# Causal attention on one core: mask, row maximum and sign folded into one VectorE instruction, transposes one unit later, PSUM copies divided between ScalarE and VectorE

## What is computed

```python
s = einsum('bhqd,bhkd->bhqk', qi, k) * scale          # FOX: + cum[t] - cum[s]
s = where(kpos <= qpos, s, -inf)
p = softmax(s, axis=-1)
out = einsum('bhqk,bhkd->bhqd', p, v)
```

## Time and profile before

| what | value |
|---|---|
| median of 3 runs | 2117.88 us |
| the profiled execution's own time | 2119.32 us |
| its span in the trace | 2117.4 us |
| PE busy over the span | 2027.0 us (96%) |
| VectorE, ScalarE, POOL busy | 988.1, 482.2, 336.7 us |
| granted PE clock, mean | 0.985 |

### The profile page before, as it was taken

The page is one execution under the profiler, slowest core; times in us unless marked ns, Lnnn a source line. Parts: engine busy times, 40 slices in busy tenths (PEclk is TensorE's granted clock), DMA queues, the critical chain, the costliest instruction groups (busy, mean ns, idle before and its releaser), DMA issues. The chain is left out here.

```text
span 2117.4 us, 20496 instructions
## 1 busy us (share of the span) xinstructions
PE 2027.0 (96%) x7494; PEld 1086.0 (51%) x7494; DVE 988.1 (47%) x1833; ACT 482.2 (23%) x1142; POOL 336.7 (16%) x474
## 2 busy tenths in 40 slices
PE   8999999999999999999899999999998999999995
PEld 4444444579874445444445456454445556544442
DVE  2444544557672124333454656253344467534333
ACT  1111111023341001100331147220004447520000
POOL 1000000001011000333100013103331003203333
PEclk9999999999999999999999999999999999999998
DMA  5223365510022124799636830138994120045996
GB/s 187 87 97 129 119 250 185 210 52 1 1 90 90 61 80 159 266 402 403 240 113 213 312 136 1 44 141 320 405 391 147 62 102 1 3 158 203 371 377 253
DMA packets 123511, 363.30 MB, mean 172 GB/s; under 512 B 27597, under 2 KB 33001, under 8 KB 110865
## 3 DMA queue, kind: packets, MB, share of 16 engines
q1 hardware_dynamic: 77856, 174.13, 23.4%
q10 hardware_dynamic: 30432, 157.30, 18.9%
q0 software_dynamic: 15120, 30.53, 4.1%
HBM read 335.60 MB, written 43.52 MB: 179 GB/s over the span
## 5 line engine op out<-in xcount | busy, mean ns | idle before, releaser
L1617 PE MATMUL bank<-ring,work 128*128 128x512 f32 x768 | 342.5, 599 | 3.3 <-DVE work L1633 3.3
L1617 PEld LDWEIGHTS bank<-ring,work 128*128 128x128 f32 x768 | 143.8, 192 | 168.1 <-issue 168.1
L1916 POOL DMA_INDIRECT work<-x_rows,small x168 | 169.2, 1007 | 269.8 <-DVE work L1881 197.3
L1628 PE MATMUL bank<-ring_halves,work 128*128 128x512 f32 x384 | 172.8, 593 | 4.0 <-DVE work L1642 4.0
L432 PE MATMUL bank<-featT,ring 128*128 128x512 f32 x384 | 170.4, 597 | 2.4 <-DMA ring<-in_w_in 2.4
L1345 PE MATMUL bank<-ring,work 128*128 128x512 f32 x384 | 168.2, 598 | 3.3 <-PEq L2182 2.2
L2396 PE MATMUL bank<-ring,featT 128*128 128x512 f32 x384 | 169.0, 601 | 1.6 <-DVE small L2485 1.6
L1639 DVE TENSOR_TENSOR work<-work,bank 128x256 f32<-128x256 f32 x48 | 20.2, 421 | 282.3 <-ACT work L1636 282.3
L2396 PEld LDWEIGHTS bank<-ring,featT 128*128 128x128 f32 x384 | 73.6, 193 | 93.9 <-issue 92.2
L1628 PEld LDWEIGHTS bank<-ring_halves,work 128*128 128x128 f32 x384 | 72.7, 190 | 95.1 <-issue 95.1
L1345 PEld LDWEIGHTS bank<-ring,work 128*128 128x128 f32 x384 | 72.8, 192 | 92.5 <-issue 92.5
(11 more groups left out here) (443 smaller groups left out, 2808.1 us busy)
## 6 DMA issues: line engine op xcount, KB each, us to landing
ring<-in_w_in SPq DMA_DIRECT2D x15, 2048.0 KB
ring<-in_moe_w_gate ACTq DMA_DIRECT2D x28, 1024.0 KB
ring<-in_moe_w_up ACTq DMA_DIRECT2D x28, 1024.0 KB
ring_halves<-in_moe_w_down ACTq DMA_DIRECT2D x28, 1024.0 KB, 10.3
ring_halves<-in_w_ada SPq DMA_DIRECT2D x48, 512.0 KB, 6.3
y_rows<-work ACTq DMA_DIRECT2D x48, 512.0 KB
ring<-in_expert_w_gate ACTq DMA_DIRECT2D x14, 1024.0 KB
ring<-in_expert_w_up ACTq DMA_DIRECT2D x14, 1024.0 KB
```

The costliest lines, as they stand in the source:

```text
L1617: last = nc.tensor.matmul(gu_sum[par], xgT[par][:, k, :], w_gu[par][:, k, :, :], start=(k == 0), stop=(k == KD - 1))
L1628: last = nc.tensor.matmul(bank[5 + h][:, :], hT[par][:, k, :], w_dn[par][:, k, span(h)], start=(k == 0), stop=(k == KF - 1))
L1916: nc.gpsimd.indirect_dma_start(out=xg[par][:, s * QD:(s + 1) * QD], out_offset=None, in_=x_quarters, in_offset=bass.IndirectOffsetOnAxis(a ...
```

## The change

The first VectorE instruction now does all three things: it adds a 512-column mask (zeros, then the triangle) to all the scores, multiplies by -1 (FOX) or by minus the row factor (MLA), writes the result back to PSUM and gives its minimum as accumulator output. ScalarE's exponent takes the scale -1.0 in both. turn moves from 3 to 4 units behind S, ScalarE's copy pT from step i + 1 to step i + 3, and the ring of pT from 4 to 6. The two long units' pT (t = 3) and the out copy go to VectorE. pv(j) moves to step 2j + 7, out(p) to 8p + 16. ScalarE's copy of a turned q stands one step before its PE step instead of two.

```diff
-        N_SX, N_PT = 6, 4
+        N_SX, N_PT = 6, 6
-            mask = scr[:, N_PT * BANK:N_PT * BANK + P]
+            mask = scr[:, N_PT * BANK:(N_PT + 1) * BANK]
-            TURN_LAG = 3
-            AHEAD = TURN_LAG - 1
+            TURN_LAG = 4
+            AHEAD = 1
+            KEEP_LAG = 3
-            pv_at = {2 * j + 5: j for j in range(N // 2)}
-            out_at_step = {PER_PAIR * p + 10: p for p in pairs}
+            pv_at = {2 * j + 7: j for j in range(N // 2)}
+            out_at_step = {PER_PAIR * p + 16: p for p in pairs}
+            by_dve = [t == T - 1 for _, t in units]
+            pT_kept = lambda j: DV if by_dve[j] else AC
...
@@ PE
-                                AC.wait(pe, ("pT", j - 2))
+                                pT_kept(j - 2).wait(pe, ("pT", j - 2))
...
@@ ScalarE
-                            DV.wait(act, ("neg" if q_root is None else "scaled", i))
+                            DV.wait(act, ("neg", i))
-                                                         scale=1.0 if q_root is None else q_root[:, at:at + 1], accum_out=inv[:, i:i + 1]), ("exp", i))
+                                                         scale=-1.0, accum_out=inv[:, i:i + 1]), ("exp", i))
-                        if 1 <= i < N + 1:
-                            j = i - 1
+                        if KEEP_LAG <= i < N + KEEP_LAG and not by_dve[i - KEEP_LAG]:
+                            j = i - KEEP_LAG
...
@@ VectorE
-                            DV.done(nc.vector.tensor_tensor(d, d, mask, ALU.add), ("mask", i))
-                            DV.wait(dve, ("mask", i))
-                            DV.done(nc.vector.reduce_max(mx[:, i:i + 1], bank[i % N_S][:, 0:(t + 1) * P], X_AXIS, negate=True), ("neg", i))
-                            if q_root is not None:
-                                at = t * NHB + h
-                                DV.wait(dve, ("neg", i))
-                                DV.done(nc.vector.tensor_tensor(mx[:, i:i + 1], mx[:, i:i + 1], q_root[:, at:at + 1], ALU.mult), ("scaled", i))
+                            DV.done(nc.vector.tensor_tensor_reduce(scores, scores, mask[:, (T - 1 - t) * P:T * P], -1.0 if minus_root is None else minus_root[:, at:at + 1],
+                                                                   3.0e38, ALU.add, ALU.min, mx[:, i:i + 1]), ("neg", i))
+                        if i in out_at_step:
+                            p = out_at_step[i]
+                            PE.wait(dve, ("pv", T * p + T - 1))
+                            DV.done(nc.vector.tensor_copy(outT[:, p, :], bank[6 + p % 2][:, :]), ("out", p))
...
+                        if TURN_LAG <= i < N + TURN_LAG and by_dve[i - TURN_LAG]:
+                            j = i - TURN_LAG
...
+                            DV.done(nc.vector.tensor_copy(pT[j % N_PT][:, 0:n, :], bank[4 + j % 2][:, 0:n * P].rearrange("p (s n) -> p s n", s=n)), ("pT", j))
```

More of the change, by code:

```diff
@@ L2137, in build, with attention @@
         TURNED_HEADS = 4
-        N_SX, N_PT = 6, 4
-        def attention(dk, q, k, v, turned_at, out_at, q_root, k_gain):
+        N_SX, N_PT = 6, 6
+        def attention(dk, q, k, v, turned_at, out_at, minus_root, k_gain):
             scr = featT[:, :, :].rearrange("p k s -> p (k s)")
@@ L2175, in attention @@
                 ac_n += [("exp", i)] if i < N else []
-                ac_n += ([("q", q_at[i + AHEAD])] if i + AHEAD in q_at else []) + ([("out", out_at_step[i])] if i in out_at_step else [])
-                ac_n += [("pT", i - 1)] if 1 <= i < N + 1 else []
+                ac_n += ([("q", q_at[i + AHEAD])] if i + AHEAD in q_at else [])
+                ac_n += [("pT", i - KEEP_LAG)] if KEEP_LAG <= i < N + KEEP_LAG and not by_dve[i - KEEP_LAG] else []
                 dv_n += [("k", k_at[i])] if i in k_at else []
-                dv_n += ([("mask", i), ("neg", i)] + ([] if q_root is None else [("scaled", i)])) if i < N else []
-                dv_n += [("inv", i - 1)] if 1 <= i < N + 1 else []
+                dv_n += [("neg", i)] if i < N else []
+                dv_n += ([("out", out_at_step[i])] if i in out_at_step else []) + ([("inv", i - 1)] if 1 <= i < N + 1 else [])
+                dv_n += [("pT", i - TURN_LAG)] if TURN_LAG <= i < N + TURN_LAG and by_dve[i - TURN_LAG] else []
             stage(pe_n, ac_n, dv_n, ["mask0", "mask"] + [("share", i) for i in range(N)])
@@ L2223, in _ @@
                             p, t = j // T, j % T
-                            AC.wait(pe, ("pT", 2 * j + 1))
+                            for m in range(2):
+                                pT_kept(2 * j + m).wait(pe, ("pT", 2 * j + m))
                             if t == 0 and p >= 2:
-                                AC.wait(pe, ("out", p - 2))
+                                DV.wait(pe, ("out", p - 2))
                             for s in range(t + 1):
@@ L2289, in _ @@
                             DV.done(nc.vector.reciprocal(inv[:, i - 1:i], inv[:, i - 1:i]), ("inv", i - 1))
+                        if TURN_LAG <= i < N + TURN_LAG and by_dve[i - TURN_LAG]:
+                            j = i - TURN_LAG
+                            n = units[j][1] + 1
+                            PE.wait(dve, ("turn", j))
+                            if j >= N_PT:
+                                PE.wait(dve, ("pv", (j - N_PT) // 2))
+                            DV.done(nc.vector.tensor_copy(pT[j % N_PT][:, 0:n, :], bank[4 + j % 2][:, 0:n * P].rearrange("p (s n) -> p s n", s=n)), ("pT", j))
                 @block.gpsimd
@@ L2294, in _ @@
                     PO.wait(pool, "mask0")
-                    PO.done(nc.gpsimd.affine_select(out=mask, in_=mask, compare_op=ALU.is_ge, fill=-3.0e38, base=0, pattern=[[-1, P]], channel_multiplier=1), "mask")
+                    PO.done(nc.gpsimd.affine_select(out=mask[:, (T - 1) * P:T * P], in_=mask[:, (T - 1) * P:T * P], compare_op=ALU.is_ge, fill=-3.0e38, base=0,
+                                                    pattern=[[-1, P]], channel_multiplier=1), "mask")
                     for i, (h, t) in enumerate(units):
@@ L2916, in _ @@
                 AC.wait(dve, "q_exp")
-                DV.done(V.scalar_tensor_tensor(out=T4(q_root, NHB), in0=T4(q_root, NHB), scalar=QK ** -0.5, in1=per_t(q_inv), op0=ALU.mult, op1=ALU.mult), "q_root")
+                DV.done(V.scalar_tensor_tensor(out=T4(q_root, NHB), in0=T4(q_root, NHB), scalar=-QK ** -0.5, in1=per_t(q_inv), op0=ALU.mult, op1=ALU.mult), "q_root")
             @block.gpsimd
```

10 lines of the change are left out of this document (3 added, 7 removed).

## The result

The changed kernel takes 2097.73 us (median of 5 runs, 2096.70 to 2103.16) against 2117.88 us. The medians differ by 20 us, where 14.5 were forecast. Over all runs the ratio is 0.9912, 95% interval 0.9896 to 0.9929, and by it the change is worth 18.6 us (15.0 to 22.0).

What follows compares the result with a forecast made beforehand. PE was taken to set the pace, with waits of 0.69 us (FOX) and 1.05 (MLA) a pair; 4.8 + 7.4 + 1.4 + 1.6 + 0.8 - 1.5 = 14.5 us off 2117.88 gave 2103.4 us, range 2098.5 to 2110.

Steps and rivals of the forecast that it cites:

- forecast case: Both attentions: PE's waits on share go, 14.5 us off the median to 2103.4 us; chance 0.72.
- low end of the range: Whole kernel at 2098.5: accumulator for nothing and no new wait, 3 us, and 1 to 2 for small waits not counted.
- Waits of pairs 1 to 7: PE's waits on share in FOX and MLA pairs, 0.69 and 1.05 us each, all gone: 4.8 and 7.4 us.
- What removes them: Share chain: the turn a unit later gives 1.45 us more cover against waits of at most 0.64.
- the tie on ScalarE: ScalarE's queue: pT(i - 1) waits for turn(i - 1) at PE's step i + 2, before exp(i + 1), delaying the next exponent.
- The new instruction: Fused VectorE step: 0.69 us for 512 columns, 0.75 with a factor from memory, plus 0.16 for the accumulator.
- What is late next: VectorE's second long pT copy, 4.0 us against PE's 3.9: 0.1 us a pair, 1.5 us given back.
- First pair and moved work: Block start: first-pair waits 0.7 us in each attention, work moved behind S(63) 0.8 in each; 1.4 + 1.6 us.
- Tail: Chain of unit 63 at each block's end: 0.3 us gained in FOX, 0.5 in MLA, together 0.8.
- VectorE's queue gives part back: Waits move to VectorE's copies, 0.5 us a pair, 6 us more given back: 2109.5; chance 0.15.
- VectorE becomes the bound: Fused instruction at two clocks an element, VectorE 12.8 us a FOX pair, 13.3 MLA: slower, 2124; chance 0.08.
- PE was not waiting: The 0.69 and 1.05 us are PE's own cost between unlike groups; only the ends gain: 2115.6; chance 0.05.

Runs made afterwards that it cites:

- lags alone: Kernel before with only the later turn, pT, pv and out, six pT tiles and nearer q copy; three VectorE instructions, copies on ScalarE: 2106.97 us, ratio 0.9948.
- pv by two: Changed kernel with two pv standing together at step 2j + 7 of the second, 2 groups a pair instead of 4: 2100.32 us, ratio 0.9914.
- extra pass: Changed kernel with one more VectorE maximum over the same columns, result unread, in front of every fused instruction: 2113.37 us, one run.

## Why the prediction was right or wrong

The direction and the forecast case were right. The time of 2103.4 us was 5.7 us above the median, and 4.2 us of gain were missing in the two blocks. The median lies 0.8 us under the low end of the range (2098.5); the ratio gives 2099.2. A part of the mechanism was wrong, and luck hid it: the change contained both parts that the gain needs. By its steps:

- *Waits of pairs 1 to 7*: 4.8 and 7.4 us, from 0.69 and 1.05 a pair. The pairs fell by 0.66 and 1.05, the middles by 84.39 - 79.33 = 5.1 and 87.15 - 79.18 = 8.0. The start-to-start reading, and 11.60 us as PE's own price, were right to 0.04.
- *What removes them*: wrong. The prediction gave it all to the lags and counted the fused instruction only in the tail. The lags alone leave 0.17 us a pair in FOX and 0.67 in MLA; the fused instruction is worth 8.2 us on top of them. The comparison of 1.45 us of cover with waits of at most 0.64 looked at the share chain only, though the prediction named the tie on ScalarE. With the share covered, the copy that frees the transposes' bank was late next. The tie itself was read rightly: one step of it costs 0.43 us a pair.
- *The new instruction*: 0.69 and 0.75 taken, 0.699 and 0.758 measured; accumulator 0.16 taken, 0.141 measured. VectorE's sum of 10.1 and 10.6 us a pair was too high, though: it is busy 7.95 and 7.93, since the sum counts overlapping records twice. The trace has two records for each fused instruction, so the accumulator that comes out for nothing, which the low end of the range counts on, did not occur. One and two clocks an element, as the prediction calls its two ends, no run shows: what stands behind them are the times of the earlier trace rows, and 0.699 and 0.758 lie beside the cheap ones. The 0.5 us for POOL's mask, named without a source, is 0.53 for the memset of 512 columns (at 1234.98), where that of 128 took 0.20 before (at 1238.36).
- *What is late next*: 1.5 us charged for a wait that did not come. The queue from the k copy to the end of the second long copy was put at 4.0 us; in the changed kernel it runs from 1270.94 to 1273.90, 2.96 us. I had added 0.4 for semaphores, where consecutive VectorE instructions overlap by some 0.08 us (the small record at 1272.16, behind 1271.81 + 0.43 = 1272.24; run after):

```profile
1270.94 0.75 DVE L2269 TENSOR_SCALAR work<-bank,small 65x512 f32<-65x512 f32 x1 [0.26 <-PE bank L2191]
...
1271.81 0.43 DVE L2281 CUSTOM_DVE_ANT_0 bank<-bank,featT 128x256 f32<-128x256 f32 x1
...
1272.16 0.14 DVE L2281 DVE_READ_ACCUMULATOR2_ANT small<- 128x1 f32 x1
1272.16 0.16 DVE L2289 RECIPROCAL small<-small 128x1 f32<-128x1 f32 x1
...
1272.23 0.67 DVE L2296 COPY featT<-bank 128x512 f32<-128x512 f32 x1
...
1273.23 0.67 DVE L2296 COPY featT<-bank 128x512 f32<-128x512 f32 x1
```

- *First pair and moved work*: 1.4 + 1.6 = 3.0 us forecast, 11.67 - 9.67 = 2.0 and 13.87 - 11.21 = 2.7 measured, 4.7. This is the term that missed most. The work that left this stretch is a turn of 3 blocks and a pv of 8 records, 0.33 + 0.59 = 0.9 us in each, so the waits that went are 1.1 us in FOX and 1.7 in MLA, where 0.7 and 0.7 were counted. The 0.2 us kept for VectorE's k copy did not stay, and FOX's waits were the price for MLA too, where the same wait before the first turn was 1735.45 - 1734.20 - 0.43 = 0.82 us instead of 0.56.
- *Tail*: 0.8 forecast, 0.47 + 0.55 = 1.0 measured. The 0.1 us taken for the semaphore between VectorE and the exponent is 1325.02 - 1324.93 = 0.09 in the changed kernel.

The sum is 13.0 + 4.7 + 1.0 = 18.7 against 10.7 + 3.0 + 0.8 = 14.5. The 1.5 us that the medians show beyond it lie within the scatter outside the blocks. FOX's block became shorter by 7.5 us and MLA's by 11.2, where 6 and 8.5 were forecast.

The rival *VectorE's queue gives part back* did not occur in this kernel, but in *pv by two* it is what eats the gain. The rival *VectorE becomes the bound* had the right place and the wrong price: it added up records that overlap, 12.8 us a pair, where the extra pass, which costs more than the rival's 2.7 us, gave 12.11. *PE was not waiting* is refuted by the pairs.

## What to carry to other kernels

In a pipeline written out by hand, a lag has a partner on every queue that the item passes. Here the lags as a set and the length of the VectorE step gave half the gain each, and a lag moved without its partner on the same queue (pT without the q copy) made the kernel slower. Once the bounding engine shows no gap, count its own fixed prices between unlike groups of work and put like groups together; then look again which copy has become late, since the best division of copies changed with it (the long copies and the out copy on VectorE were worth 1.4 us in the blocks before, and the long ones cost about 6 after). Take block lengths from start to start where the rest of the program scatters by more than the effect.

## What the runs showed of the hardware

- The fused instruction's minimum comes out by a second record of 0.141 us, and in the changed kernel it and a reciprocal behind it have the same start, 1272.16: records on VectorE overlap there, so their sum overstates the queue (2.96 us, idle time included, where the nine records from 1270.94 on add up to 3.54).
- PE paid 0.09 to 0.10 us in front of a group of pv (each product in one column half of the array, 128*64 in the rows) and 0.14 to 0.15 us behind it, at 4, 8, 12, 16 and 28 records: in pv by two the 28 took 1.68 us, 7 x 0.22 + 0.14. With two groups a pair in place of four, and the long copies on ScalarE, the pair fell by 0.44 us. That the halves are the cause, and not the change of operands, was not tried.
- A factor from memory cost 0.06 us in the fused instruction of 512 columns (0.758 against 0.699), and in the exponent of 512 columns 0.09: 0.78 in the lags-only kernel's MLA, and in the changed kernel's MLA, where the scale is a constant, 0.69 (below). The runs with the fused instruction have this shorter exponent in MLA too, and its part in their gain was not taken apart.

```profile
1806.80 0.69 ACT L2253 ACTIVATE ring_halves<-bank,small 128x512 f32<-128x512 f32 x1
```
